# Two layers of a hybrid attention, pooling and convolution block: a projection moved into the conditioning, and four re-timings

## The reference

```python
mods = silu(c) @ w_ada + b_ada            # sh1, sc1, g1, sh2, sc2, g2, per layer
h = rms_norm(x, g_pre1) * (1 + sc1) + sh1
u = h @ w_in                              # 2048 -> q 1024, k 256, v 256, pool 512, conv 2 x 512
mix = concat(attention(q, k, v),          # 16 heads, 4 key heads; latents also see cached keys
             pooling(pool, (2, 4, 8, 16)),
             conformer_conv(conv)) @ w_out   # glu, 31 depthwise taps, layer norm, silu, pointwise
x = x + g1 * rms_norm(mix, g_post1)
h = rms_norm(x, g_pre2) * (1 + sc2) + sh2
x = x + g2 * rms_norm(square(relu(h @ w_mlp1)) @ w_mlp2, g_post2)   # 2048 -> 8192 -> 2048
```

## Time and profile before

| | us |
|---|---|
| median of 3 runs | 3365.73 (3362.77 to 3366.11) |
| profiled execution | 3363.93 |
| its span | 3362.1 |
| PE busy | 3178.8 (95%) |
| DVE busy | 2188.4 (65%) |
| ACT busy | 1120.0 (33%) |
| POOL busy | 186.9 (6%) |

### The profile page before, as it was taken

One profiled execution on the slowest core, in us unless ns is written; L12 is line 12 of the kernel. 1 busy time (PEld: TensorE's weight loads), 2 busy tenths in 40 slices (PEclk: granted clock), 3 DMA queues, 4 the chain that ended last, 5 costly groups with the idle time before them and its releaser, 6 DMA issues.

```text
span 3362.1 us, 48664 instructions
## 1 busy us (share of the span) xinstructions
PE 3178.8 (95%) x17339; PEld 2770.8 (82%) x17339; DVE 2188.4 (65%) x3132; ACT 1120.0 (33%) x1567; POOL 186.9 (6%) x209
## 2 busy tenths in 40 slices
PE   5899899889999999999997998988999999999999
PEld 2587756788988988989886996678899899898997
DVE  1347656588889888888887597757456463434335
ACT  2122323342332323323234324434233333332332
POOL 0002023000000000000000022400000000000000
PEclk7699999989999999999998999998999999999999
DMA  9865475257666666667662432224445444444342
GB/s 303 289 205 171 156 226 168 77 178 231 216 218 203 219 221 219 207 208 233 211 210 91 126 119 66 76 76 161 160 142 176 148 156 125 132 125 131 125 130 102
DMA packets 422060, 566.28 MB, mean 168 GB/s; under 512 B 17688, under 2 KB 280464, under 8 KB 421552
## 3 DMA queue, kind: packets, MB, share of 16 engines
q1 hardware_dynamic: 419648, 560.02, 51.4%
q0 software_dynamic: 1344, 4.33, 0.4%
q10 hardware_dynamic: 944, 0.32, 0.0%
HBM read 560.93 MB, written 3.67 MB: 168 GB/s over the span
## 4 chain that ended last, share of the span: by engine, by line
PE 76%; DVE 12%; issue 5%; DMA 3%; ACT 3%; ACTq 0%; DVEq 0%; SPq 0%
PE ps L1349 39%; PE ps L1357 31%; DVE w_lo L815 3%; DVE ada_sums L1250 3%; DVE conv L1037 2%; DMA ada_raw<-in_w_ada_dram 2%; PE ps L1435 2%; PE ps L1598 1%; DMA raw<-in_w_in_dram 1%; PE ps L1572 1%; PE ps L1586 1%; ACT w_hi L543 1%; ACT facc L584 1%; PE ps L1378 1%; DVE facc L1270 0%
## 5 line engine op out<-in xcount | busy, mean ns | idle before, releaser
L815 DVE TENSOR_TENSOR w_lo<-raw,w_hi 128x1024 fp32r<-128x1024 f32 x672 | 826.3, 1233 | 779.6 <-ACT w_hi L543 759.2
L543 ACT ACTIVATE w_hi<-raw 128x1024 fp32r<-128x1024 f32 x672 | 711.0, 1059 | 1525.5 <-PE ps L1357 802.3
L1349 PE MATMUL ps<-h_hi,w_hi 128*128 128x384 f32 x2816 | 953.5, 339 | 10.3 <-DVE w_lo L815 10.3
L1349 PE MATMUL ps<-h_lo,w_hi 128*128 128x384 f32 x2816 | 945.9, 336 | 0.0
L1349 PE MATMUL ps<-h_hi,w_lo 128*128 128x384 f32 x2816 | 945.9, 336 | 0.0
L1357 PE MATMUL ps<-w_hi,hid_hi 128*128 128x512 f32 x1536 | 602.3, 392 | 19.5 <-DVE facc L1270 17.6
L1357 PE MATMUL ps<-w_hi,hid_lo 128*128 128x512 f32 x1536 | 598.8, 390 | 0.0
L1357 PE MATMUL ps<-w_lo,hid_hi 128*128 128x512 f32 x1536 | 598.6, 390 | 0.0
L1250 DVE SCALAR_TENSOR_TENSOR ada_sums<-ada_raw,cond,ada_sums 128x512 f32<-128x512 f32 x840 | 575.4, 746 | 0.0
L1349 PEld LDWEIGHTS ps<-h_hi,w_hi 128*128 128x128 f32 x2816 | 532.3, 189 | 26.8 <-issue 14.0
L1349 PEld LDWEIGHTS ps<-h_lo,w_hi 128*128 128x128 f32 x2816 | 532.4, 189 | 0.9
(11 more groups left out here) (185 smaller groups left out, 1906.4 us busy)
## 6 DMA issues: line engine op xcount, KB each, us to landing
raw<-in_w_mlp_dram SPq DMA_DIRECT2D x512, 512.0 KB, 3.8
ada_raw<-in_w_ada_dram SPq DMA_DIRECT2D x384, 512.0 KB, 4.6
raw<-in_w_in_dram SPq DMA_DIRECT2D x96, 512.0 KB, 4.8
raw<-in_w_out_dram SPq DMA_DIRECT2D x64, 512.0 KB, 3.7
out_dram<-x SPq DMA_DIRECT2D x6, 512.0 KB, 2.6
x<-in_x_sample_dram SPq DMA_DIRECT2D x1, 2048.0 KB, 10.2
pw_w<-in_w_conv_pw_dram POOLq DMA_DIRECT2D x2, 1024.0 KB, 6.7
x<-in_x_prompt_dram SPq DMA_DIRECT2D x1, 1024.0 KB, 5.3
```

The lines of the kernel that those rows point to most:

```text
L543: nc.scalar.activation(w_hi[:, j % 4, :, :], raw[:, j % 4, :, :], ACT.Copy).then_inc(hi_ready, 1)
L815: nc.vector.tensor_tensor(w_lo[:, j % 4, :, :], raw[:, j % 4, :, :], w_hi[:, j % 4, :, :].bitcast(F32), ALU.subtract).then_inc(lo_ready, 1)
L1349: last = nc.tensor.matmul(ps[:, 2 * pair + t, 0:TOK], w[:, j % 4, k, P * t:P * t + P], v[:, kt + k, :], start=begin and k == 0 and i == 0, ...
```

## The change

Five parts, all in one edit:

1. The first 512 columns of `w_in` in layer 0 are multiplied inside the first conditioning, by 8 pairs of row tiles: the ada blocks come in the order 0, 8, 1, 9, ..., in two PSUM banks in turn; after each pair one wide load of `w_in` follows, and `unit_rows` (24 matmuls) runs two blocks later, the last behind the last turn. `ADA_QKV` and `ADA_MIX` fall by two, so that two more blocks stand in layer 0's attention (`ADA_STEPS` 18 to 21).
2. `keep_warm` issues 7, 5 and 1 matmuls of constants behind the transposes of the three token tiles in a closing.
3. `WIDE_QUADS` puts the second block's second half in quad 4 instead of 5.
4. Four pieces run ahead of the wait for the keys; the cached keys are copied ahead of the keys' rotation and have a semaphore of their own; the last two steps have no pieces; ACT's evictions of pieces move with them.
5. The convolution's padded row becomes three blocks of 158, so that a tap runs over 3 x 128 elements; the sums by `ones` and the centering take 384 at once.

```diff
-ADA_CU, ADA_QKV, ADA_MIX = 16, 20, 28
+ADA_CU, ADA_QKV, ADA_MIX = 16, 18, 26
...
-WIDE_QUADS = ((1, 2), (3, 5), (6, 7))
+WIDE_QUADS = ((1, 2), (3, 4), (6, 7))
...
+CONV_BLOCK = P + 2 * C_HALF
+CONV_PAD = TT * CONV_BLOCK
...
+ADA_FIRST = (7, 6)
+X_BANKS = (4, 5)
+PAIRS = 8
...
+AHEAD = 4
...
-            for j in range(4):
-                load_ada(0, 0, j, wait=False)
-            for j in range(4):
-                load_unit(j, 0, part(w_in, 0, 512 * j, CA0 * P), wait=False)
-            with sp.Fori(1, ADA_CU) as m:
-                for j in range(4):
-                    load_ada(0, m, j)
+            for i in range(PAIRS):
+                for h, m in enumerate((i, PAIRS + i)):
+                    for j in range(4):
+                        load_ada(0, m, j, wait=2 * i + h > 0, n=2 * i + h)
+                load_wide(i % 4, i // 4, w_in, 0, 2 * P * i, CA0 * P, wait=i >= 4)
             for layer in range(DEPTH):
                 first = layer == 0
 
                 if first:
-                    for j in range(4):
-                        load_ada(0, ADA_CU, j)
-                    for j in range(4, 8):
-                        load_unit(j, 0, part(w_in, 0, 512 * (j - 4), CA0 * P + UC))
-                        load_ada(0, ADA_CU + 1, j - 4)
-                    load_blocks(0, w_in, 2, CA0 * P + 2 * UC, (0, ADA_CU + 2))
+                    load_blocks(0, w_in, 2, CA0 * P + 2 * UC, (0, ADA_CU))
...
+                    load_pair(0, 1, 0, ADA_MIX + 12)
+                    for j in range(2, 4):
+                        load_out(0, 1, j)
+                    with sp.Fori(0, 3) as i:
                         for j in range(4):
-                            load_out(i, 1, j)
+                            load_out(i + 1, 1, j)
...
-                nc.gpsimd.memset(glu[:, :, 0:C_HALF], 0.0).then_inc(pads_ready, 1)
-                nc.gpsimd.memset(glu[:, :, C_HALF + CTX:C_HALF + CONV_LAT], 0.0).then_inc(pads_ready, 1)
-                nc.gpsimd.memset(glu[:, :, C_HALF + CONV_OUT:CONV_PAD], 0.0).then_inc(pads_ready, 1)
+                nc.gpsimd.memset(glu[:, :, 0, 0:C_HALF], 0.0).then_inc(pads_ready, 1)
+                nc.gpsimd.memset(glu[:, :, 0, C_HALF + P:CONV_BLOCK], 0.0).then_inc(pads_ready, 1)
+                nc.gpsimd.memset(glu[:, :, 1, 0:C_HALF], 0.0).then_inc(pads_ready, 1)
+                nc.gpsimd.memset(glu[:, :, 2, C_HALF + P:CONV_BLOCK], 0.0).then_inc(pads_ready, 1)
...
+            for i in range(PAIRS):
+                if i >= 4:
+                    act.wait_ge(unit_used, i - 3)
+                w_high(i % 4, i // 4)
+                h_high(i)
...
-                        if i % 6 == 5:
+                        if i % 6 == 3:
                             side_copy(i // 6, 0)
                             side_copy(i // 6, 1)
+                        if i % 6 == 4:
+                            side_copy(i // 6, 2)
...
+            for i in range(PAIRS):
+                kts = slice(2 * i, 2 * i + 2)
+                for h, m in enumerate((i, PAIRS + i)):
+                    ada_copy(2 * i + h, ADA_FIRST[h])
+                    ada_mods(0, m, 2 * i + h, ADA_FIRST[h])
+                if i == 0:
+                    dve.wait_ge(x_copied, 12)
+                dve.wait_ge(mods_ready, 2 * i + 2)
...
+                nc.vector.tensor_tensor(h_lo[:, kts, :], full[:, kts, :], h_hi[:, kts, :].bitcast(F32),
+                                        ALU.subtract).then_inc(h_ready, 1)
+                w_low(i % 4, i // 4)
...
+                for block_, first_token, last_token, offset in ((0, 0, CTX, C_HALF), (1, CTX, CTX + P + C_HALF, C_HALF),
+                                                                (2, CTX + P - C_HALF, TOK, 0)):
+                    span = slice(first_token, last_token)
+                    chain.link(nc.vector.tensor_tensor(glu[:, :, block_, offset:offset + last_token - first_token],
+                                                       z[:, CA0:CA0 + 4, span], z[:, CG0:CG0 + 4, span], ALU.mult))
...
-                    src, out, w = glu[:, t, k:k + CONV_OUT], conv[:, t, :], pc[:, layer, c:c + 1]
+                    src, out = glu[:, t, :, k:k + P], conv[:, t, :].rearrange("p (b n) -> p b n", n=P)
+                    w = pc[:, layer, c:c + 1]
...
-                    nc.vector.tensor_tensor(act_in[:, :, 0:CTX], conv[:, :, 0:CTX], per_token(rstd, 4, 0, CTX), ALU.subtract)
-                    nc.vector.tensor_tensor(act_in[:, :, CTX:TOK], conv[:, :, CONV_LAT:CONV_OUT], per_token(rstd, 4, CTX, TOK),
-                                            ALU.subtract).then_inc(cen_ready, 1)
+                    nc.vector.tensor_tensor(act_in[:, :, :], conv[:, :, :], per_token(rstd, 4), ALU.subtract).then_inc(cen_ready, 1)
...
+                def copy_cached_keys():
+                    dve.wait_ge(conv_act, layer + 1)
+                    dve.wait_ge(ck_turned, layer + 1)
+                    for a in range(2):
+                        for b in range(2):
+                            last = nc.vector.tensor_copy(kdv[64 * b:64 * b + 64, :, a, TOK:512],
+                                                         ps[64 * a:64 * a + 64, 6, 0:256].rearrange("p (t n) -> p t n", n=P))
+                    last.then_inc(ck_taken, 1)
...
-                after[7] = list(after[7]) + [pool_low, rope_keys, copy_keys]
+                after[7] = list(after[7]) + [pool_low, copy_cached_keys, rope_keys, copy_keys]
...
+            def keep_warm(n, bank):
+
+                for i in range(n):
+                    nc.tensor.matmul(ps[:, bank, :], ident[:, :], cond[:, :, :].rearrange("p a b -> p (a b)"), start=True, stop=True)
...
+                    if t == 0:
+                        pe.wait_ge(mods_ready, (ADA_BLOCKS, ADA_BLOCKS + ADA_WIDE - 1, ADA_BLOCKS + ADA_WIDE)[p - 1])
+                        keep_warm(7, BANK_ADA)
+                    else:
+                        pe.wait_ge(f_added, 12 * p)
+                        keep_warm(5 if t == 1 else 1, BANK_ACC + 2)
...
+            def unit_rows(u):
+
+                pe.wait_ge(lo_ready, u + 1)
+                pe.wait_ge(h_ready, u + 1)
+                for k in range(2):
                     for t in range(4):
-                        last = nc.tensor.transpose(ps[:, 2 + g % 2, P * t:P * t + P], facc[:, place(j), b, P * t:P * t + P], ident[:, :])
-                    last.then_inc(x_turned, 1)
-                ada_turn(m)
-            with pe.Fori(4, ADA_CU) as m:
-                for j in range(4):
-                    ada_unit(m, j)
-                ada_turn(m)
+                        for i, (w, v) in enumerate(((w_hi, h_hi), (w_hi, h_lo), (w_lo, h_hi))):
+                            last = nc.tensor.matmul(ps[:, t, 0:TOK], wide(w, u)[:, k, P * t:P * t + P], v[:, 2 * u + k, :],
+                                                    start=u == 0 and k == 0 and i == 0, stop=u == PAIRS - 1 and k == 1 and i == 2)
+                last.then_inc(unit_used, 1)
+
+            for n in range(2 * PAIRS):
+                ada_unit(n, 0, ADA_FIRST[n % 2], n - 1)
+                if n:
+                    ada_turn(n - 1, ADA_FIRST[(n - 1) % 2], n - 2)
+                for j in range(1, 4):
+                    ada_unit(n, j, ADA_FIRST[n % 2], n - 1)
+                if n == 0:
+                    turn_rows()
+                if n < 3:
+                    for g in range(4 * n, 4 * n + 4):
+                        turn_first_x(g)
+                if n >= 3 and n % 2 == 1:
+                    unit_rows(n // 2 - 1)
+            ada_turn(2 * PAIRS - 1, ADA_FIRST[1], 2 * PAIRS - 2)
+            unit_rows(PAIRS - 1)
...
-                    two_blocks(0, 0, ADA_CU, lambda j: pe.wait_ge(h_ready, 2 * j + 2))
-                    two_blocks(2, 2, ADA_CU + 2)
+                    two_blocks(2, 2, ADA_CU)
...
-                    for a, b, src in ((0, CTX, 0), (CTX, TOK, CONV_LAT)):
-                        for t in range(4):
-                            last = nc.tensor.matmul(ps[:, BANK_SUM, a:b], ones[:, :], conv[:, t, src:src + b - a], start=t == 0, stop=t == 3)
+                    for t in range(4):
+                        last = nc.tensor.matmul(ps[:, BANK_SUM, 0:TOK], ones[:, :], conv[:, t, :], start=t == 0, stop=t == 3)
...
-                        side_piece(2 * i)
+                        if 2 * i + AHEAD < 48:
+                            side_piece(2 * i + AHEAD)
...
-                        side_piece(2 * i + 1)
+                        if 2 * i + 1 + AHEAD < 48:
+                            side_piece(2 * i + 1 + AHEAD)
...
+                pe.wait_ge(v_ready, 2 * (layer + 1))
+                pe.wait_ge(ck_taken, layer + 1)
+                for piece in range(AHEAD):
+                    side_piece(piece)
```

More of the change, by code:

```diff
@@ L1023, in _ @@
[L1023 to L1024 removed]
+                if first:
+                    for j in range(4):
+                        w_low(j, 2)
+                    eight_units(2, *ada_pair(0, ADA_CU))
+                else:
```

(2 more changed lines are left out.)

147 lines of the change are left out of this document (61 added, 86 removed).

## The result

The changed kernel takes 3339.82 us (median of 4 runs, 3339.02 to 3340.83), the kernel before 3365.92 in the same comparison: a ratio of 0.9925, interval 0.9913 to 0.9937. The forecast was 3313, and the range, 3295 to 3334, does not hold the time.

A forecast was written before the change was run, and what follows sets the result against it. PE bound the 3362.1 us span, so gains had to come where PE waits or is clocked low. -12 - 3 - 24 - 9.5 - 4.5 = -53 gave 3310.9; the median lies 1.8 higher: 3313, range 3295 to 3334.

The forecast's parts named there:

- Part A: First conditioning: input projection by rows between ada blocks, less two blocks moved into layer 0's attention: -12 (-3 to -19).
- the pace of the loads: First conditioning: three more loads at 1.75 us move the last ada matmul 5.3 us, plus 1.5 for pauses, to 137.8.
- The tail after it: Conditioning's end: from the last ada matmul at 137.8 to the second 512 columns starting at about 156.2.
- Rival One: First conditioning becomes bound by PE at the low clock; Part A becomes +7, total 3332; chance 13%.
- The two blocks moved into layer 0's attention: Layer 0's attention: two ada blocks leaving the projection cost 3.1 us each, +6.2.
- Part B: Closings: matmuls of constants keep PE's clock up while it waits: -3 (+4 to -7).
- Half of the loss: Closings: of the 6 to 7 us lost to low clock, half is won back: -3.
- Part C: Layer 0's MLP chunks: products in other quads remove stalls on DVE's adds: -24 (-4 to -27).
- Part D: Both attentions: four pieces fill PE's idle time ahead of the first scores: -9.5 (-14 to -2).
- Rival Three: Attention's end and closings: pieces are given back (-2), constants don't keep the clock (0); total 3323; chance 11%.
- Part E: Convolution in both layers: taps over 384 instead of 414 elements: -4.5 (0 to -8).
- two at once: Whole kernel: two rivals together, left out of the range with the slower rival; under 2 in 10 with the bounds' remainder.

The follow-up runs named there:

- small parts: The changed kernel with each row unit's 24 matmuls cut into eight parts of 3, the last half unit behind the last turn: 3324.62 us, ratio 0.9877.
- a third: The changed kernel with only the high by high products in the row units, 8 matmuls instead of 24: 3317.8 us in one run.

## Where the prediction was right and wrong

**Part A: wrong, in one step.** The step that failed is the pace of the loads: "three more loads come ahead of it: 3 x 1.75 = 5.3 us", and 1.5 us "for pauses after the new waits". The last ada matmul was to end at 137.8 and ended at 153.70. The tail after it came as reckoned in sum: 18.4 us forecast, 172.22 - 153.70 = 18.5 measured. The loads were counted as if SP could always issue them. But a load waits for its ada buffer, a buffer comes free when PE has used it, and there are four; a row unit on PE stops the issue for up to 6.7 us. So a pair took 17.6 us, where 9 x 1.75 = 15.8 was reckoned and 14.7 is what the loads alone can do: 9 of the 16 us in five pairs. About 7 lie ahead of them: by the sixth block the loads were 3.7 us later than before and should have been two loads, 3.5 us, earlier. The wait of 4.94 us at 46.12 is in that stretch, and the kernels with small parts and with a third have it too (4.84 and 4.94); no run undoes it.

Rival One's sign was loads "more than 1.8 us apart"; they are 17.6/9 = 1.96. It had PE full at the low clock. In the changed kernel PE was busy 74% of these pairs, at 0.77, and waited for loads in between, so that is not the whole of it. But the clock is part of it: at 0.80 the small parts were no faster than whole units. How the 2 us a pair divide between the length of a hold and the clock stays open. The rule weighed there (the Trainium skill, "TensorE: Matmul & The Clock Gate", section "HAM oscillation — how this bites in real kernels": bursts behind a wait on DMA begin throttled) agrees with the trace in that the six row units from 66.20 to 153.70 took 5.4 to 6.6 us and not 4.3, their first records 0.52 us long and the later ones 0.33.

The two blocks moved into layer 0's attention cost 6.4 us between the first and the last score beside part D, against +6.2 forecast, but 3.0 in the two kernels without part D (158.6 and 155.6 us); their size is not settled.

**Part B: about right, as far as the runs tell.** -3 forecast; undone, the time did not change, and the two stages that were read lost 0.5 and 1.3 us. "Half of the loss" was a coin toss between idle times of like length. In the trace the clock of the closing was mostly held (0.94 of full speed in the first, against 0.60 before), and the 1.95 us just ahead of the stage still cost the ten slow matmuls. With that wait filled as well the loss is gone.

**Part C: right.** -24 forecast, 21.0 in layer 0's MLP, 18.9 to 22.3 by undoing it. A chunk gained 2.54 and not 3.1, and the last 2.2, where 2 was forecast. That the stall was DVE's is shown by the waits, 17.6 us before and 2.6 now.

**Part D: wrong, beyond its bounds.** -9.5 forecast with -14 to -2 as bounds; undone, the kernel is 3.4 us faster by the medians and 5.6 by the spans, so it brings nothing and likely costs some us. The step that failed is "so part of the moved work returns as a wait: 1.3 to 2.5 us a layer". It looked at the distance of scores, 4.1 us, as the limit of a step without pieces. The limit lies elsewhere: a transposition waits for DVE's `o_sb`, a mix for `prob_t`, and a piece is what PE does meanwhile. So nearly the whole of the 4.97 us that was filled ahead came back: in layer 1 the waits after the last score grew from 3.1 to 5.8 us, and 1.75 came just ahead of it. Rival Three named the place and had it at -2.

**Part E: right.** -4.5 forecast; 4.6 us of span and 6.0 of time when undone; five taps in 2.65 us.

**The sum and the range.** By the medians, undoing a part gives A -0.6, B -0.3, C +22.3, D -3.4, E +6.0, together 24, and the whole is 26 below the kernel before, so the parts add up within what the times can tell. By the spans of single executions it is -3.1, +2.3, +18.9, -5.6 and +4.6, together 17 of 23.5. In layer 0, from the sums to the closing, part D costs more beside the two moved blocks (8.1 us with both, 1.5 with the blocks alone, -1.0 with part D alone) than the waits explain; the clock is where it shows. Of the 27 us between forecast and result nearly all are A and D, some 13 each. The range failed since what rivals One and Three stand for came together, and "two at once" was left out, under 2 in 10 with the rest. They are of one kind, and that ought to have raised the chance of both: each says that a gap is not free to be filled, or work not free to be taken away, since a buffer or a chain of another engine hangs on it.

## What to carry to other kernels

Where an engine frees the buffers of a stream, work put between its uses can be paid in transfers, even when neither the engine nor the transfers are full; ask of such work how long the stream can go without a free buffer. Here the row units in eight parts, half a unit of them moved behind the last turn, turned a part worth nothing into 14 to 17 us. About half of the gain was the move (whole units with unit 6 moved gave 8.9 us, about 5.5 of them by the move), and the shorter pairs were those in which the clock stayed up, so that cutting alone helps is not shown. Before moving filler out of a loop, ask which latency it covers there: a loop in which the engine never waits can still be one in which the filler is what keeps it from waiting. To keep a clock over a pause, fill its last piece, too.

## What the runs showed of the hardware that was not expected

The clock fell 1.2 us after work had begun again, not in the pause: after 1.95 us of idle time at 689 to 691, records were 0.33 us long from 691.3 to 692.2 and 0.53 from there to 695.1. So the cost of a pause can stand in rows behind it that look busy. And wide loads of 2 KB rows cost no more than ada loads of 1 KB rows: one wide and eight ada loads took 14.7 us at a DMA share of 0.99, 1.63 a load, against 1.75 at 0.95 for ada loads alone.
